# Last head of a mixer: result tiles loaded and split together, output units begun two steps earlier, additions to x put behind each step's own work

## The reference

```python
h = rms_norm(x, norm1_gain) * (1.0 + sc1) + sh1
proj = h @ w_in                                  # 4096 columns, cut into q, f, v, gate, lx, lg
o_f, s_f = hgrn2_chunkwise(q[0], logf[0], v, s0)           # 4 heads, key and value width 128
o_b, s_b = hgrn2_chunkwise(flip(q[1]), flip(logf[1]), flip(v), s0)
hg_out = rms_norm(o_f + flip(o_b), hg_norm_gain) * silu(hgate)
xc = dwconv_centred(lx, conv_w, conv_b)                    # width 4
r, i = sigmoid(block_diag(xc, wa, ba)), sigmoid(block_diag(xc, wx, bx))
a = exp(-8 * r * softplus(-lam)); u = sqrt(1 - a * a) * (i * xc)      # then scan h = a h + u
lru_out = (h_f + flip(h_b)) * gelu(lg)
x = x + g1 * (concatenate([hg_out, lru_out]) @ w_out)
x = x + g2 * (square(relu(h2 @ w_ff1)) @ w_ff2)            # h2 from x as h above
y = rms_norm(x, final_gain)
```

## Time and profile before

| | |
|---|---|
| median of three runs | 1821.04 us |
| the profiled execution | 1818.81 us |
| its span, first to last instruction | 1817.0 us |
| PE busy | 1707.3 us, 94% |
| DVE busy | 918.4 us, 51% |
| ACT busy | 542.2 us, 30% |
| mean granted TensorE clock | 0.964 |
| DMA | 155.63 MB, mean 86 GB/s |

### The profile page before, as it was taken

How to read it: one execution, slowest core, us unless ns; L and a number is a source line. 1 busy time by engine, 2 the same in 40 slices (tenths; PEclk the granted TensorE clock), 3 DMA queues, 4 the chain that set the end, 5 groups by cost and what they waited for, 6 DMA issues and landing times. The chain is left out here.

```text
span 1817.0 us, 30963 instructions
## 1 busy us (share of the span) xinstructions
PE 1707.3 (94%) x13176; PEld 1440.9 (79%) x13176; DVE 918.4 (51%) x1364; ACT 542.2 (30%) x794; POOL 0.2 (0%) x4
## 2 busy tenths in 40 slices
PE   7799999899989995999799999999999999999996
PEld 5587787678778874887688888888888888888885
DVE  5703634643555267446755544455444454544455
ACT  3512327322813463253341122111122111222103
POOL 0000000000000000000000000000000000000000
PEclk7899999999999997999799999999999999999998
DMA  8444324322523436110111011111011110011103
GB/s 331 194 171 141 113 79 164 129 97 72 205 99 111 145 129 257 58 47 13 58 47 47 1 47 47 46 46 37 10 46 46 46 46 17 30 46 46 35 1 127
DMA packets 42788, 155.63 MB, mean 86 GB/s; under 512 B 6848, under 2 KB 11456, under 8 KB 41408
## 3 DMA queue, kind: packets, MB, share of 16 engines
q1 hardware_dynamic: 37648, 132.91, 20.9%
q10 hardware_dynamic: 5040, 21.22, 2.9%
HBM read 118.19 MB, written 35.92 MB: 85 GB/s over the span
## 5 line engine op out<-in xcount | busy, mean ns | idle before, releaser
L1598 DVE SCALAR_TENSOR_TENSOR x<-bank,mod,x 128x512 f32<-128x512 f32 (+1 forms) x384 | 246.1, 660 | 145.7 <-PE bank L97 144.4
L95 PE MATMUL bank<-h_hi,in_lo 128*128 128x512 f32 (+1 forms) x768 | 288.6, 376 | 12.0 <-issue 8.2
L95 PE MATMUL bank<-h_hi,up_lo 128*128 128x512 f32 (+1 forms) x768 | 272.9, 355 | 8.8 <-DVE h_lo L398 6.3
L96 PE MATMUL bank<-h_lo,in_hi 128*128 128x512 f32 (+1 forms) x768 | 275.7, 359 | 0.0
L97 PE MATMUL bank<-h_hi,in_hi 128*128 128x512 f32 (+1 forms) x768 | 275.5, 359 | 0.0
L96 PE MATMUL bank<-h_lo,up_hi 128*128 128x512 f32 (+1 forms) x768 | 272.8, 355 | 0.0
L97 PE MATMUL bank<-h_hi,up_hi 128*128 128x512 f32 (+1 forms) x768 | 272.2, 354 | 0.0
L96 PE MATMUL bank<-hid_lo,down_hi 128*128 128x256 f32 x720 | 256.1, 356 | 0.0
L95 PE MATMUL bank<-hid_hi,down_lo 128*128 128x256 f32 x720 | 255.5, 355 | 0.0
L97 PE MATMUL bank<-hid_hi,down_hi 128*128 128x256 f32 x720 | 254.6, 354 | 0.0
L95 PEld LDWEIGHTS bank<-h_hi,in_lo 128*128 128x128 f32 x768 | 147.4, 192 | 38.5 <-issue 15.0
(11 more groups left out here) (199 smaller groups left out, 2012.4 us busy)
## 6 DMA issues: line engine op xcount, KB each, us to landing
proj<-mx_stage ACTq DMA_DIRECT2D x32, 640.0 KB, 5.4
up_raw<-in_w_ff SPq DMA_DIRECT2D x34, 512.0 KB, 5.7
in_raw<-in_w_in SPq DMA_DIRECT2D x32, 512.0 KB, 5.9
mx_ada_raw<-in_w_ada_rest SPq DMA_DIRECT2D x32, 512.0 KB, 4.8
down_raw<-in_w_ff SPq DMA_DIRECT2D x30, 512.0 KB, 3.3
ada<-in_w_ada SPq DMA_DIRECT2D x8, 1024.0 KB, 20.6
x_scratch<-x_first SPq DMA_DIRECT2D x1, 5120.0 KB, 17.6
mx_f<-proj SPq DMA_DIRECT2D x8, 640.0 KB, 7.1
```

The lines of the kernel that those rows point to most:

```text
L95: nc.tensor.matmul(out, w_lo, x_hi, start=start, stop=False)
L96: nc.tensor.matmul(out, w_hi, x_lo, start=False, stop=False)
L1598: nc.vector.scalar_tensor_tensor(xs, g.bank[3 + u % DOWN_BANKS][:, 0:n], g.m(40 + m, int(b > 0)), xs, ALU.mult, ALU.add).then_inc(unit_add ...
```

## The change

The six result tiles are all loaded at step 4, ahead of the last head's own loads, instead of three at step 4 and three at step 6. The splits of tiles 1 to 5 all stand in step 6, ahead of that step's own work. `S_EARLY` goes from 8 to 6: u0 stands ahead of the half blocks of 32, and the 24 units are spread over 18 steps, not 16. On DVE, the additions to x (and the low halves of the next weights) move from the start of a step to its end, behind `mix`, through a new argument of `turns`.

```diff
-SPLIT_AT = {4: (0,), 5: (1, 2), 6: (3, 4), 7: (5,)}
-S_EARLY = 8
+SPLIT_AT = {5: (0,), 6: (1, 2, 3, 4, 5)}
+S_EARLY = 6
...
-        def turns(eng, project, mix, out, half=None):
+        def turns(eng, project, mix, out, half=None, finish=None):
...
                 mix(HEADS - 1, step)
+                if finish is not None:
+                    finish(step)
...
-                for i in {LEAD: (0, 1, 2), LEAD + 2: (3, 4, 5)}.get(step, ()):
-                    sp.dma_start(early_raw[:, i, :], g.mix_out[EARLY[i], :, :]).then_inc(early_in[i], 16)
+                    for i in range(6):
+                        sp.dma_start(early_raw[:, i, :], g.mix_out[EARLY[i], :, :]).then_inc(early_in[i], 16)
...
-                for i in SPLIT_AT.get(step - 1, ()):
+                for i in SPLIT_AT.get(step, ()):
                     act.wait_ge(early_in[i], 16)
...
+            def add_early(step):
+                for u in early_units(step):
+                    m, b = divmod(u, 3)
+                    if b == 0 and m + 1 < KT:
+                        out_weights(m + 1)
+                    if u in (0, 3):
+                        dve.wait_ge(x_in[u // 3], 16)
+                    dve.wait_ge(early_full, u + 1)
+                    add_to_x(u, u % 2, early_added)
+
             def out(step):
...
-                for u in early_units(step):
-                    m, b = divmod(u, 3)
-                    if b == 0 and m + 1 < KT:
-                        out_weights(m + 1)
-                    if u in (0, 3):
-                        dve.wait_ge(x_in[u // 3], 16)
-                    dve.wait_ge(early_full, u + 1)
-                    add_to_x(u, u % 2, early_added)
...
-            turns(dve, project, mix, out)
+            turns(dve, project, mix, out, finish=add_early)
```

## The result

The changed kernel takes 1843.3 us (median of four runs, 1842.0 to 1844.4) beside 1821.2 us for the kernel before (four runs, 1820.8 to 1825.9). The ratio is 1.0128, with a 95% interval of 1.0108 to 1.0147. The forecast was 1842.6 us. The profiled execution took 1843.12 us, with a span of 1841.3 and a mean granted clock of 0.960.

The account below looks back on a forecast made before the run. PE was taken as full from u0 on, with DVE setting u0's start. Terms -7.1 + 2.3 + 2.0 + 20.95 + 3.4 = +21.6 us on 1821.04 gave 1842.6 us, range 1834 to 1850.

Parts of the forecast that it names:

- u0 earlier: Start of the last head's early units: DVE's reordered splits let u0 start at 722.0 instead of 729.14, 7.1 us gained.
- half blocks in the full stretch: Half blocks of 32 and 64 now stand in PE's full stretch: 0.9 and 1.4 us, 2.3 us lost.
- u2's wait: PE ahead of u2: u0's addition stands behind second weights whose load queues behind x; 2.0 us wait.
- waits of u12, u15, u16, u19, u20: PE behind steps 14 to 20: additions queued behind DVE's step work hold these units 3.3, 4.5, 9.1, 2.0, 3.0 us.
- wait ahead of u17 gone: PE ahead of u17: the old 0.95 us wait goes, since its addition is long done.
- clock: PE behind its new gaps: two losses of granted clock at 1.7 us each, 3.4 us.
- its upper bound of 8.5 us: Clock term's upper bound: 1.7 us lost at each of u2, u12, u15, u16 and u20.
- The additions stay hidden: Rival for the early units: banks are free in time, only start and half blocks count; -5.8, 1815.3 us; chance 6%.
- In part overlapped: Rival: u15, u16, u19 and u20 each lose 2 us less and the clock holds; +10.2, 1831 us; chance 10%.
- Loads are late: Part of a rival: crowded queue delays u0 up to 2 us, plus three more clock losses; about 1850 us; chance 7%.

Follow-up runs that it names:

- e5: The changed kernel with unread matmuls filling PE's waits ahead of u15, u16 and u20 (13, 30 and 10): 1834.76 us, ratio 1.0091.
- e2: The kernel before with only the additions to x moved behind mix: 1845.95 us, ratio 1.0142.
- e10: The changed kernel with additions behind mix in steps 6, 7 and 17 only, elsewhere at the step's start: 1822.84 us, ratio 1.0023.
- e4: The changed kernel with additions behind mix in steps 6 and 7 only, later at the step's start: 1815.38 us, ratio 0.9979.
- e3: The changed kernel with three PSUM banks for the early units instead of two: 1816.24 us, ratio 0.9984.
- e6: The kernel before with only the loads changed, all six result tiles at step 4: 1820.93 us, ratio 1.0004.
- e1: The changed kernel with the additions to x back at the start of every step: 1818.42 us, ratio 0.9997.
- e8: The changed kernel with additions behind mix only in steps 6 and 7, three banks, half blocks of 32 ahead of u0: 1812.23 us, ratio 0.9964.

## Why the prediction was right

By its own steps. Lengths of units are from the first matmul to the next group.

| step | predicted | measured |
|---|---|---|
| u0 earlier | -7.1 | -7.10 |
| half blocks in the full stretch | +2.3 | 1.22 + 1.32 = +2.5 |
| u2's wait | +2.0 | 0 (0.65 in e5) |
| waits of u12, u15, u16, u19, u20 | 3.3, 4.5, 9.1, 2.0, 3.0 | 3.16, 4.19, 8.49, 1.95, 3.22 |
| wait ahead of u17 gone | -0.95 | -0.95 |
| clock | +3.4 | +6.0, and -1.3 |
| sum | +21.6 | +20.2, of +21.6 in the stage |

**The five waits** came where they were placed, each to about 0.6 us, in sum 21.0 of 21.9. The way to get them was the right one: take the time from PE's last matmul of a step to DVE's last work of it, and subtract what PE still has to do. e2 had five waits forecast in the same way and met them to 0.7 us, and e10 shows the largest alone. Of the 1.4 us that the sum lacks, most lies in how idle time is counted: from the end of PE's last matmul, while the next one could have started sooner. The group at 814.38 lasts 2.31 us, but where nothing waits the unit behind such a group starts 1.75 us after its start (828.67 to 830.42 in e5). So u16 was held up by 825.18 - 816.13 = 9.05 us rather than 8.49, closer still to the 9.1; at u15, u19 and u20, behind units, the same count adds 0.2 us each.

**The half blocks** ran as priced, one at half clock. In PE's timeline:

```profile
727.33 1.30 PE L1103 MATMUL bank<-mx_q,mx_k 128*32 128x32 f32 x80
728.55 0.62 PE L95 MATMUL bank<-mx_early_hi,mx_out_lo 128*128 128x512 f32 x1
...
733.00 1.39 PE L1114 MATMUL bank<-mx_q,mx_k 128*64 128x64 f32 x40
734.32 0.50 PE L95 MATMUL bank<-mx_early_hi,mx_out_lo 128*128 128x512 f32 x1
```

**u2's wait was mis-sized, its mechanism was there.** The second weights did queue behind x: issued at 723.10, their load landed 8.1 us later, where 3.4 us are usual, and 1.1 us behind x. Their high half on ACT begins at 731.23, predicted 731.5.

```profile
731.23 1.06 ACT L966 ACTIVATE mx_out_hi<-mx_out_raw 128x1024 fp32r<-128x1024 f32 x1 [15.98 <-DMA mx_out_raw<-in_w_out]
```

DVE then made the low half and added u0:

```profile
732.33 1.23 DVE L1399 TENSOR_TENSOR mx_out_lo<-mx_out_raw,mx_out_hi 128x1024 fp32r<-128x1024 f32 x1
733.47 0.48 DVE L1406 SCALAR_TENSOR_TENSOR x<-bank,mod,x 128x256 f32<-128x256 f32 x1
```

The addition ended at 733.95, and PE was through with the second half blocks at 734.3, so there was nothing left to wait for. Counted from each trace's own mark, the addition was ready after 19.5 us where the prediction had 21.0 (the weights landed 1.5 us sooner than my guess behind x), and PE was free after 19.9 us where it had 19.1, because the half blocks of 32 and the start of u1 still ran at half clock. A predicted wait of 1.9 us became a margin of 0.4. Two smaller things lie in this. The prediction's own terms for PE add up to 732.5 or 732.6, not 732.4, a slip of 0.1 to 0.2 us. And 1.3 of the 1.5 us come from x itself: the prediction left its load at 710.99, 2.3 us ahead of the mark, but with no result tiles to issue at step 6 SyncE issued it at 709.92, 4.5 us ahead of the mark.

e5 shows how thin the margin is. Its code is that of after up to u14, but there the lower clock ended sooner, within u0 instead of behind the half blocks of 32, PE was ready earlier, and u2 did wait for u0's addition:

```profile
733.82 0.50 PE L95 MATMUL bank<-mx_early_hi,mx_out_lo 128*128 128x512 f32 x1 [0.65 <-DVE x L1412]
```

**The clock was mis-sized the other way.** Two losses of 1.7 were taken; there were three, 1.5, 2.8 and 1.6. u16 lost most: 12 of its 18 matmuls started 0.43 us apart, where full clock gives 0.23. Against that, a fall that the kernel before had at u9 was absent: its 18 small matmuls took 3.5 us there (778.15 to 781.66), against 2.2 us in the kernel after (773.32 to 775.56). The errors of size, 2.0 us too much at u2 and 0.9 at the waits, 1.3 too little at the clock and 1.4 that no term holds, cancel by luck; the forecast came closer than its terms.

The Trainium skill, "TensorE: Matmul & The Clock Gate", section "Why this matters for your kernels", warns that longer idle gaps between bursts of matmuls send the engine back to half rate. The trace agrees at u15, u16 and u20, and not at u12, where 3.16 us of idle time cost nothing; nor did the 1.95 us ahead of u19, which the page's row may not mean. Charging all five gaps that the prediction listed, its upper bound of 8.5 us, would have made the sum 5 us too high.

**The rivals.** "The additions stay hidden" forecast 1815.3 us and failed in the kernel after, at the point that the prediction named: DVE's work of a step ended later than PE's next unit. Where the additions stand ahead of the long steps it comes near: in e4 the stage is 5.6 us shorter than before, where the rival had 5.8, though 1.3 of the 5.6 are the fall of the clock at u9 that e4 lacks, and the time is 0.21% (3.8 us) lower. The Trainium skill, page "Perfetto Trace Analysis", section "Matmuls", says that groups of matmuls should rotate through PSUM banks, so that the emptying of one overlaps with the next. With two banks and the additions last it did not (21.0 us of waits), with three it nearly did (2.9 us, e3). "In part overlapped" wanted four waits 2 us shorter than forecast; none was shorter by more than 0.6 us. "Loads are late" failed: u0 came 8.77 us after the mark, no split waited for a tile, and e6 shows no cost of the loads.

## What to carry to other kernels

An operation that frees a buffer should not stand behind work of its engine that itself waits for the engine that wants the buffer. Before such a move, measure from the last matmul of the step to the last work of it, and subtract what the waiting engine still has to do: that gave five waits to about 0.6 us, and five others in e2 to 0.7. Where the order cannot be changed, one more buffer does the same (18 of 21 us here), and it pays to choose the order step by step: in steps 6 and 7 the additions and the low weights ahead of them were better last (e4 against e1, 6.1 us in the stage), from step 14 on better first.

## What the runs showed of the hardware that was not expected

Idle time and the clock go together loosely. A gap of 3.16 us (u12) and one of 1.95 us (u19) cost nothing, one of 3.22 us (u20) cost 1.6 us, one of 4.19 us (u15) 1.5 us. In e3 a gap of 2.89 us (u17) cost 1.6 us too, so the length of a gap alone does not decide. At u20 the slow stretch did not even begin with the restart: matmuls start every 0.23 us up to 851.62 and every 0.43 us from 851.95 on, 1.6 us into the unit.

```profile
850.69 0.39 PE L96 MATMUL bank<-mx_early_lo,mx_out_hi 128*128 128x512 f32 x1
...
851.95 0.63 PE L95 MATMUL bank<-mx_early_hi,mx_out_lo 128*128 128x512 f32 x1
852.38 0.63 PE L96 MATMUL bank<-mx_early_lo,mx_out_hi 128*128 128x512 f32 x1
```

Unread matmuls in a wait kept the clock up (e5), at no cost that showed; each group ended before its wait did, with 1.25, 1.66 and 0.97 us left. And the clock sometimes falls without an idle gap, behind step 13's twenty matmuls of one column: at u9 in the kernel before and in e6, at u10 in e5 and e8, and not in after, where u10 follows the same group. What decides that was not tested. Nor were two gaps of 3.4 to 4.7 us in the scores of level 4, which every trace shows and puts down to no other engine.
